# Reordering TensorE's work behind the state update of a hybrid DeltaNet and window-attention layer

## The chip, the cores and the metric

The kernel runs on one core of one Trainium2 chip. The metric is the device time of one execution in microseconds (us). Engines are named as in the profile: PE is TensorE (PEld its weight loads), DVE is VectorE, ACT is ScalarE, POOL is GpSimd, and SP issues most of the DMAs.

## What is computed

```python
h = rmsnorm(x, pre_norm_w)                      # x: 4096 rows of 1024, float32
proj = einsum('bsd,de->bse', h, w_in)           # 3336 columns
(qa, ka, va, za, ba, aa, qb, kb, vb, zb) = split(proj)
qkv = silu(causal_depthwise_conv(concat([qa, ka, va]), conv_w))
o_a = gated_deltanet(...)                       # 4 heads of 128, chunks of 64, state 128x128 a head
o_a = rmsnorm(o_a, dn_out_norm_w) * silu(za)
o_b = sliding_window_sink_attention(...)        # 8 heads of 64, window of 2 chunks
o_b = o_b * silu(zb)
y = einsum('bse,ed->bsd', concat([o_a, o_b]), w_out)
out = x + rmsnorm(y, post_norm_w)
```

## The kernel before

The 4096 rows are taken in 32 tiles of 128 rows (two chunks of 64). `run_steps` unrolls 33 steps for every engine; step t projects tile t (`proj`, the "fill") and mixes tile m = t - 1 (`mix`: DeltaNet, attention, output projection). It also prepares the x of tile t + 1 (`prep`). So step 0 has no mixing, steps 2 to 30 have all three parts, step 31 has a projection but no x to prepare, and step 32 has mixing alone. Step 1 (m = 0) also splits `w_out` into its half-precision parts, on ACT and DVE (`w_out_high`, `w_out_low`).

Each engine has its own program, and the order in it is written out by hand; engines meet at semaphores. `done(engine, event, n)` is a wait until `event` has come for tile n. On PE the work that depends on other engines is spread between pieces of the projection: `fill(n)` issues the next n of 26 pieces of tile t. A piece of the kind that matters here is 24 matmuls of 128 columns (L500), 8 chunks of the contraction by three products of high and low half-precision parts. The last four pieces are the columns of the DeltaNet queries (`FILL_Q`); their end releases `conv_fill` on ACT (L782 to L786), which feeds DVE's convolution of the queries (L1050, L1052), ACT's tanh (L792) and DVE's SiLU (L1061).

The end of a step on PE, in the order of the program (L680 to L718):

- the products of the state update: `per_head(2, k_tail, cw, ds_ready)` and `per_head(7, decay, cw, aw_ready)`, L515;
- `fill(2)`, then the output projection of group B's half: 24 matmuls of 512 columns into banks 4 and 5 (L692, from `out_b_half`);
- the four turns (transposes) of group A's normalised output `mt` into bank 3 (L708), which wait for `on_ready`; then `gate_columns` (L572);
- `fill(2)`, then `turn_x(t + 1)`: 16 turns of the high and low halves of the next x (L435), the second eight of which wait for `xl_ready`;
- the output projection of group A's half (L692, from `out_a_half`, whose buffer is `inv_t`), which waits for `out_a_ready` and signals `y_ready`.

`on_ready` is made by a chain over three engines that begins when the state update's products end: DVE adds the two parts of the output into `mt` (L1356); ACT squares and sums it per head (L947); DVE forms the argument (L1364, L1366); POOL takes the power (L1596), multiplies the four factors (L1598) and scales `mt` (L1600). Beside this chain DVE goes on in its own order: the last tap of the keys' convolution (L1052), then `low_half(t + 1)` (L1018, one pass over 1024 columns with two inputs in SBUF), then the gate of group B (L1069).

`out_a_ready` is made from the turned output: DVE multiplies by the gate (L1380), ACT copies to half precision (L957), DVE subtracts (L1387). In ACT's order `conv_fill(FILL_Q)`, the copy of the turned x (L752) and the queries' tanh come behind L957, and behind them the squares of the output projection (L966), which wait for `y_ready`. These lead over POOL (L1602 to L1606) to `y_rs` and to `finish` on DVE (L1400) in the next step.

At m = 0 one part of `w_out` (its chunk 4) lies for a while in the buffer `y_out`; DVE moves it away and signals `wo_ready` (L1031), and SP then loads the first rows of x into `y_out` (L407).

Of the kernel before, what the change touches and what calls it, by code (L numbers as in the profile page):

```python
# [87 lines left out]
def build(nc, x, pre_norm_w, w_in, conv_w, dn_a_log, dn_dt_bias, dn_out_norm_w, sw_sinks, w_out,  # L88
# [7 lines left out]
    with ExitStack() as ctx:  # L96
# [64 lines left out]
        out_b_half = sb("out_b_half", [128, 2, 4, 128], F16)  # L161
# [198 lines left out]
        @block.sync  # L360
        def _(sp):
            sp.dma_start(x_in[:, :], x[0, 0:TOK, :]).then_inc(x_loaded, 16)
            sp.dma_start(c32[:, :, :], const32).then_inc(const_loaded, 16)
            sp.dma_start(rows[0:48, :], conv_w[0].rearrange("k (b p) -> (k b) p", p=128)).then_inc(const_loaded, 16)
            sp.dma_start(rows[48:56, :], pre_norm_w[0].rearrange("(c p) -> c p", p=128)).then_inc(const_loaded, 16)
            sp.dma_start(rows[56:57, :], dn_out_norm_w).then_inc(const_loaded, 16)
            sp.dma_start(masks[:, :, :], const16).then_inc(const_loaded, 16)
            for c in range(NC):
                r = slice(128 * c, 128 * c + 128)
                for at, lo, hi in ((COL_Q, 0, 1536), (COL_ZA, 1536, 2048), (COL_QB, 2056, 2824),  # L370
                                   (COL_ZB, 2824, 3336), (COL_KVB + 256, 2048, 2056)):
                    sp.dma_start(w_raw[:, c + 1, at:at + hi - lo], w_in[0, r, lo:hi]).then_inc(w_loaded[c], 16)
            done(sp, xh_ready, 0)
            sp.dma_start(x_in[:, :], x[0, TOK:2 * TOK, :]).then_inc(x_loaded, 16)
            for c in range(NC):
                sp.dma_start(w_o[:, c, :], w_out[0, 128 * c:128 * c + 128, :]).then_inc(wo_loaded, 16)

            def step(t, p, mix, proj, prep):
                m = t - 1
                if mix:  # L380
                    done(sp, near_ready, m)
                    done(sp, xl_ready, t - 1 if proj else m - 1)
                    sp.dma_start(near_dram, m_near.rearrange("p h n -> p (h n)")).then_inc(near_stored, 16)
                    sp.wait_ge(near_stored, (m + 1) * 16)
                    sp.dma_start(x_in[:, 0:BLOCK * 4 * BLOCK],
                                 near_dram.rearrange("(b j) n -> b (j n)", j=BLOCK).unsqueeze(1).broadcast_to(
                                     [128 // BLOCK, BLOCK, 4 * BLOCK * BLOCK])).then_inc(block_loaded, 16)
                    sp.wait_ge(block_loaded, (m + 1) * 16)
                if proj:
                    done(sp, q_rot_ready, m)  # L390
                    sp.dma_start(rot_tab[:, :], rotary[bass.ds(t * TOK, TOK), :]).then_inc(rot_loaded, 16)
                if mix and m:
                    done(sp, post_ready, m - 1)
                    sp.dma_start(out[0, bass.ds((m - 1) * TOK, TOK), :], y_out[:, :]).then_inc(stored, 16)
                    sp.wait_ge(stored, m * 16)
                    sp.dma_start(y_out[:, :], x[0, bass.ds(m * TOK, TOK), :]).then_inc(res_loaded, 16)
                if not mix:
                    sp.wait_ge(w_hi_ready, 2 * NC)
                    sp.wait_ge(w_lo_ready, LOW_PARTS * NC)
                    done(sp, fill_ready[FILL_Q], 0)  # L400
                    sp.dma_start(post_w, post_norm_w.broadcast_to([128, D])).then_inc(pw_loaded, 16)
                if prep and mix:
                    done(sp, to_ready, m)
                    sp.dma_start(x_in[:, :], x[0, bass.ds((t + 1) * TOK, TOK), :]).then_inc(x_loaded, 16)
                if m == 0:
                    sp.wait_ge(wo_ready, 1)
                    sp.dma_start(y_out[:, :], x[0, 0:TOK, :]).then_inc(res_loaded, 16)  # L407

            run_steps(sp, step)
            done(sp, post_ready, NT - 1)  # L410
            sp.dma_start(out[0, bass.ds((NT - 1) * TOK, TOK), :], y_out[:, :]).then_inc(stored, 16)
            sp.wait_ge(stored, NT * 16)
# [3 lines left out]
        def _(pe):  # L416
# [8 lines left out]
            def turn_x(n):  # L425

                done(pe, xh_ready, n)
                done(pe, w_ready, n - 2)
                done(pe, o_ready, n - 2)
                for s in range(2):  # L430
                    if s:
                        done(pe, xl_ready, n - 1)
                    dst = bank[6 + s][:, :].bitcast(F16).rearrange("p (c n) -> p c n", c=NC)
                    for c in range(NC):
                        last = nc.tensor.transpose(dst[:, c, :], x_split(n)[:, s, 128 * c:128 * c + 128], ident16)  # L435
                last.then_inc(x_turned, 1)
# [38 lines left out]
            def step(t, p, mix, proj, prep):  # L475
                m = t - 1
# [3 lines left out]
                def fill(n, ahead=False):  # L480

                    nonlocal asked, issued
                    if not proj:
                        return
                    asked += 0 if ahead else n
                    while issued < (n if ahead else asked):
                        issued += 1
                        f, b = next(queue)
                        dst = bank[(p + f) % 2]
                        if (f, b) == (0, 0):  # L490
                            turned_x(pe, t)
                        if b == 0 and t == 1 and f < 2:
                            done(pe, fill_used[FIRST_USER[f]], 0)
                        elif b == 0:
                            done(pe, fill_used[(f - 2) % 7], t if f >= 2 else m)
                        if f in FILL_COL:
                            col = FILL_COL[f] + 128 * b
                            for c in range(NC):
                                for ws, xs in ((0, 0), (0, 1), (1, 0)):
                                    last = mm(dst[:, 128 * b:128 * b + 128], w_half[:, c, ws, col:col + 128],  # L500
                                              xt_half[:, xs, c, :], start=(c == 0 and ws + xs == 0),
                                              stop=(c == NC - 1 and ws == 1))
                        else:
                            col, n_col, per = (COL_QB, 512, NC // 4) if f == FILL_QB else (COL_KVB, KV, NC // 2)
                            for c in range(per * b, per * b + per):
                                for xs, ws in ((0, 0), (0, 1), (1, 0)):
                                    last = mm(dst[:, 0:n_col], xt_half[:, xs, c, :],  # L507
                                              w_half[:, c, ws, col:col + n_col], start=(c == 0 and ws + xs == 0),
                                              stop=(c == NC - 1 and xs == 1))
                        if (f, b + 1) not in PIECES:  # L510
                            last.then_inc(fill_ready[f], 1)
# [171 lines left out]
                done(pe, w_ready, m)  # L683
                per_head(2, k_tail, cw, ds_ready)
                per_head(7, decay, cw, aw_ready)
                fill(2)

                def project_out(chunks, src, begin, event=None):
                    for i, c in enumerate(chunks):
                        for xs, ws in ((0, 0), (0, 1), (1, 0)):  # L690
                            for n in range(2):
                                last = mm(bank[4 + n][:, :], src[:, xs, i, :],  # L692
                                          w_out_half(c, m)[:, ws, 512 * n:512 * n + 512],
                                          start=(begin and i == 0 and xs + ws == 0),
                                          stop=(not begin and i == len(chunks) - 1 and xs == 1))
                    if event is not None:
                        last.then_inc(event, 1)

                if m == 0:
                    pe.wait_ge(wo_lo_ready, 4)  # L700
                if m == 1:
                    pe.wait_ge(wo_ready, 1)
                project_out(range(4, 8), out_b_half, True)

                done(pe, on_ready, m)
                done(pe, qs_used, m)
                for h in range(4):
# [1 line left out]
                last.then_inc(o_turned, 1)  # L709
                if proj:  # L710
                    gate_columns(t)
                fill(2)
                if prep:
                    turn_x(t + 1)
                done(pe, out_a_ready, m)
                if m == 0:
                    pe.wait_ge(wo_lo_ready, NC)
# [955 lines left out]
```

## Time and profile before

| | |
|---|---|
| median of 3 runs | 2083.33 us (2082.55 to 2083.40) |
| span of the profiled execution | 2082.3 us |
| PE busy | 2008.8 us, 96% |
| PEld busy | 1666.1 us, 80% |
| DVE busy | 1612.2 us, 77% |
| ACT busy | 998.3 us, 48% |
| POOL busy | 525.7 us, 25% |
| DMA | 93.02 MB, mean 45 GB/s |

The profile is of one execution, whose span is 2082.3 us; the page gives no other time for it, and the median of the runs is 1.0 us above the span. A busy share counts the time in which an instruction of the engine is under way. The ends of matmuls are modelled, and the record of one overlaps the next by some tenths of a microsecond, so the beginning of the next instruction tells more than the recorded end. The chain that ended last, and the list of what ran at which time, show the order inside a step.

### The profile page before, as it was taken

The numbers are of one execution on the slowest core, as the hardware profiler recorded it, in microseconds if no ns is written. First come the engines' busy times: TensorE is split into PE (matmuls) and PEld (weight loads), VectorE is DVE, ScalarE is ACT, GpSimd is POOL, SyncE is SP. The second block draws the span as 40 slices with busy tenths as digits, with TensorE's granted clock in tenths as the row PEclk, the third lists the DMA queues.
The fourth block names the chain that finished last, engine by engine and source line by source line (L and its number), as shares of the span: only waits on it lengthen the run. The fifth ranks groups of instructions, "written<-read, shape, count | busy, mean of one in ns | idle before, by whom it ended". The sixth has DMA issues, their size and how long they took to land.

```text
span 2082.3 us, 61176 instructions
## 1 busy us (share of the span) xinstructions
PE 2008.8 (96%) x24913; PEld 1666.1 (80%) x24913; DVE 1612.2 (77%) x5455; ACT 998.3 (48%) x3144; POOL 525.7 (25%) x809
## 2 busy tenths in 40 slices
PE   7589999999999999999999999999999999999985
PEld 7568888888888888888878878888888888888873
DVE  6888777788777778777777877777877777887773
ACT  6655444545454544444454545454544444454532
POOL 0222222222222222222223222222222222322221
PEclk9799999999999999999999999999999999999996
DMA  9001100111110011110011111011111001111100
GB/s 359 27 23 54 44 24 23 43 45 44 44 34 23 33 44 44 44 44 24 23 43 44 44 44 34 18 38 44 44 44 41 19 30 44 45 44 44 33 10 34
DMA packets 35530, 93.02 MB, mean 45 GB/s; under 512 B 9209, under 2 KB 13618, under 8 KB 35250
## 3 DMA queue, kind: packets, MB, share of 16 engines
q1 hardware_dynamic: 34818, 89.11, 13.0%
q8 instruction: 197, 3.23, 0.7%
q14 instruction: 83, 0.68, 0.1%
q10 hardware_dynamic: 432, 0.01, 0.0%
HBM read 71.28 MB, written 17.83 MB: 43 GB/s over the span
## 4 chain that ended last, share of the span: by engine, by line
PE 89%; DVE 5%; ACT 3%; DMA 2%; issue 1%; SPq 0%; POOL 0%; POOLq 0%; ACTq 0%; DVEq 0%
PE bank L500 39%; PE bank L692 16%; PE bank L507 11%; PE bank L515 10%; PE bank L660 2%; PE bank L649 1%; PE bank L636 1%; DMA x_in<-near_scratch 1%; PE bank L435 1%; DVE w_raw L1435 1%; PE bank L555 1%; PE bank L532 1%; PE bank L537 1%; ACT w_raw L978 1%; PE bank L588 1%
## 5 line engine op out<-in xcount | busy, mean ns | idle before, releaser
L500 PE MATMUL bank<-xt_half,w_raw 128*128 128x128 f16 x14880 | 904.9, 219 | 9.6 <-ACT xt_half L752 9.6
L500 PEld LDWEIGHTS bank<-xt_half,w_raw 128*128 128x128 f16 x14880 | 863.6, 98 | 31.7 <-issue 15.5
L1052 DVE SCALAR_TENSOR_TENSOR qkv<-conv_in,cols,qkv 128x128 f32<-128x128 f32 x1152 | 391.8, 384 | 3.5
L507 PE MATMUL bank<-w_raw,xt_half 128*128 128x264 f16 (+1 forms) x1488 | 261.9, 330 | 2.0 <-DVE w_raw L1069 2.0
L507 PEld LDWEIGHTS bank<-w_raw,xt_half 128*128 128x128 f16 x1488 | 145.1, 98 | 87.1 <-DVE w_raw L1069 2.2
L692 PE MATMUL bank<-w_o,inv_t 128*128 128x512 f16 x768 | 172.7, 382 | 2.7 <-DVE inv_t L1387 2.7
L692 PE MATMUL bank<-w_o,out_b_half 128*128 128x512 f16 x762 | 169.7, 379 | 0.0
L692 PEld LDWEIGHTS bank<-w_o,inv_t 128*128 128x128 f16 x768 | 74.1, 98 | 87.5 <-DVE inv_t L1387 3.1
L1050 DVE TENSOR_SCALAR qkv<-conv_in,cols 128x128 f32<-128x128 f32 x384 | 90.9, 282 | 64.3 <-ACT halo L786 63.0
L692 PEld LDWEIGHTS bank<-w_o,out_b_half 128*128 128x128 f16 x762 | 73.2, 98 | 82.7
L752 ACT ACTIVATE xt_half<-bank,small 128x128 f16<-128x128 f16 x496 | 131.7, 418 | 3.8 <-DVE small L1479 3.6
L1142 DVE TENSOR_TENSOR masks<-x_in,base_inv 128x60 f32<-128x60 f32 (+14 forms) x480 | 108.9, 227 | 17.6 <-DMA x_in<-near_scratch 4.5
L1146 DVE TENSOR_TENSOR base_inv<-base_inv,masks 128x60 f32<-128x60 f32 (+14 forms) x480 | 106.3, 221 | 15.4
L792 ACT ACTIVATE tanh_c<-qkv 128x512 f32<-128x512 f32 x96 | 60.5, 630 | 113.4 <-DVE qkv L1052 113.3
L1602 POOL TENSOR_TENSOR small<-small 128x1 f32<-128x1 f32 x32 | 6.3, 196 | 404.7 <-ACT work L966 404.7
L1544 POOL TENSOR_TENSOR q_rot<-shared,rot_tab 128x512 f32<-128x512 f32 x32 | 41.4, 1294 | 224.1 <-ACT shared L825 224.1
L1380 DVE TENSOR_TENSOR bank<-bank,w_raw 128x512 f32<-128x512 f32 x32 | 22.4, 699 | 96.0 <-PE bank L708 96.0
L1596 POOL TENSOR_TENSOR small<-small 128x4 f32<-128x4 f32 x32 | 33.8, 1057 | 240.2 <-DVE small L1366 240.2
L782 ACT ACTIVATE conv_in<-halo 128x12 f32<-128x12 f32 x96 | 20.1, 209 | 153.1 <-PE bank L500 153.1
L1061 DVE SCALAR_TENSOR_TENSOR qkv<-tanh_c,qkv 128x512 f32<-128x512 f32 x96 | 66.1, 689 | 34.2 <-ACT tanh_c L792 34.1
L957 ACT ACTIVATE inv_t<-bank 128x512 f16<-128x512 f32 x32 | 19.1, 597 | 151.8 <-DVE bank L1380 151.8
L906 ACT ACTIVATE shared<-bank,small 128x128 f32<-128x128 f32 x256 | 89.6, 376 | 0.0
(257 smaller groups left out, 3546.0 us busy)
## 6 DMA issues: line engine op xcount, KB each, us to landing
x_in<-in_x_dram SPq DMA_DIRECT2D x32, 512.0 KB, 3.3
x_in<-near_scratch SPq DMA_DIRECT2D x32, 512.0 KB
y_out<-in_x_dram SPq DMA_DIRECT2D x32, 512.0 KB, 3.2
out_dram<-y_out SPq DMA_DIRECT2D x32, 512.0 KB, 2.9
w_raw<-in_w_in_dram SPq DMA_DIRECT2D x8, 768.0 KB, 10.8
w_raw<-in_w_in_dram SPq DMA_DIRECT2D x16, 256.0 KB, 10.9
w_o<-in_w_out_dram SPq DMA_DIRECT2D x8, 512.0 KB, 12.8
w_raw<-in_w_in_dram SPq DMA_DIRECT2D x8, 384.0 KB, 10.9
```

The lines of the kernel that those rows point to most:

```text
L500: last = mm(dst[:, 128 * b:128 * b + 128], w_half[:, c, ws, col:col + 128], xt_half[:, xs, c, :], start=(c == 0 and ws + xs == 0), stop=(c ...
L507: last = mm(dst[:, 0:n_col], xt_half[:, xs, c, :], w_half[:, c, ws, col:col + n_col], start=(c == 0 and ws + xs == 0), stop=(c == NC - 1 a ...
L515: last = mm(bank[b][:, 128 * h:128 * h + 128], lhs[:, h, :], right[:, h, :] if len(right.shape) == 3 else right, start=start, stop=stop)
L692: last = mm(bank[4 + n][:, :], src[:, xs, i, :], w_out_half(c, m)[:, ws, 512 * n:512 * n + 512], start=(begin and i == 0 and xs + ws == 0) ...
L752: last = f(xt_half[:, s, c, :], src[:, c, :], ACT.Identity, scale=x_factor[:, c:c + 1])
L792: f(tanh_c[:, :], qkv[:, 4 * g:4 * g + 4, :].rearrange("p h n -> p (h n)"), ACT.Tanh, scale=0.5).then_inc(tanh_c_ready[g], 1)
L906: last = f(soft[:, hh, :], heads(4 + hh // 4)[:, hh % 4, :], ACT.Exp, scale=DH_B ** -0.5, bias=row_max[:, hh:hh + 1], accum_out=row_sum[:, ...
L1050: last = v.tensor_scalar(dst, conv_in[:, b, 0:TOK], tap, None, ALU.mult)
L1052: last = v.scalar_tensor_tensor(dst, conv_in[:, b, i:i + TOK], tap, dst, ALU.mult, ALU.add)
L1061: v.scalar_tensor_tensor(y, tanh_c[:, :], 1.0, y, ALU.add, ALU.mult).then_inc(qkv_ready[g], 1)
L1142: link(v.tensor_tensor(x_prod[:, :, 0:k], m_block[:, 0:k, :, k].rearrange("p j h -> p h j"), base_inv[:, :, k:k + 1].broadcast_to([128, 4, ...
L1146: link(v.tensor_tensor(base_inv[:, :, 0:k], base_inv[:, :, 0:k], x_prod[:, :, 0:k], ALU.subtract))
```

## The change

PE's order at the end of a step is rewritten. All four last pieces of the projection stand directly behind the state update's products; then come the turns of group A's output, `gate_columns` and `turn_x`; both output projections stand last, one behind the other. Since group B's projection of m = 0, which reads `y_out`, now stands behind the turns, SP's load into `y_out` waits in addition for `y_ready` of tile 0.

```diff
                 if m == 0:
                     sp.wait_ge(wo_ready, 1)
+                    done(sp, y_ready, 0)
                     sp.dma_start(y_out[:, :], x[0, 0:TOK, :]).then_inc(res_loaded, 16)
...
                 per_head(7, decay, cw, aw_ready)
-                fill(2)
+                fill(4)
...
+                done(pe, on_ready, m)
+                done(pe, qs_used, m)
+                for h in range(4):
+                    last = nc.tensor.transpose(heads(3)[:, h, :], mt[:, h, :], ident)
+                last.then_inc(o_turned, 1)
+                if proj:
+                    gate_columns(t)
+                if prep:
+                    turn_x(t + 1)
                 if m == 0:
                     pe.wait_ge(wo_lo_ready, 4)
                 if m == 1:
                     pe.wait_ge(wo_ready, 1)
                 project_out(range(4, 8), out_b_half, True)
-
-                done(pe, on_ready, m)
-                done(pe, qs_used, m)
-                for h in range(4):
-                    last = nc.tensor.transpose(heads(3)[:, h, :], mt[:, h, :], ident)
-                last.then_inc(o_turned, 1)
-                if proj:
-                    gate_columns(t)
-                fill(2)
-                if prep:
-                    turn_x(t + 1)
                 done(pe, out_a_ready, m)
```

PE before, at the end of a step with all three parts. `xt_half` is the turned x, `w_raw` holds the weights, `out_b_half` and `inv_t` hold the halves of the mixed output, `mt` is group A's output before it is turned:

```order
L515 MATMUL bank<-cw,decay 128x128 x4
L500 MATMUL bank<-xt_half,w_raw 128x128 x48
L692 MATMUL bank<-w_o,out_b_half 128x512 x24
L708 MATMUL bank<-c,mt 128x128 x4
L572 MATMUL bank<-small,c 128x4
L500 MATMUL bank<-xt_half,w_raw 128x128 x48
L435 MATMUL bank<-masks,shared 128x128 x16
L692 MATMUL bank<-w_o,inv_t 128x512 x24
L588 MATMUL bank<-c,small 128x128 x4
```

And PE at the same place in the changed kernel, with the semaphores that stand ahead of an instruction (a group is then split at its first instruction):

```order
L516 MATMUL bank<-cw,decay 128x128 x4
L501 MATMUL bank<-xt_half,w_raw 128x128 [waits conv_in_ready1]
L501 MATMUL bank<-xt_half,w_raw 128x128 x95
L703 MATMUL bank<-c,mt 128x128 [waits qs_used,on_ready]
L703 MATMUL bank<-c,mt 128x128 x3
L573 MATMUL bank<-small,c 128x4 [waits state_ready,g_ready]
L436 MATMUL bank<-masks,shared 128x128 [waits o_ready,w_ready,xh_ready]
L436 MATMUL bank<-masks,shared 128x128 x7
L436 MATMUL bank<-masks,shared 128x128 [waits xl_ready]
L436 MATMUL bank<-masks,shared 128x128 x7
L693 MATMUL bank<-w_o,out_b_half 128x512 [waits wo_ready]
```

Between the state update and the turns of `mt` there are now 96 fill matmuls, where there were 48 and the 24 wide matmuls of group B's projection; that projection now stands behind all turns and directly ahead of group A's.

SP at m = 0, in the changed kernel; before, the row of `y_out` waited for `wo_ready` alone:

```order
L391 DMA rot_tab<-in_rotary_dram 128x128 [waits q_rot_ready,block_loaded]
L404 DMA x_in<-in_x_dram 128x1024 [waits base_made]
L408 DMA y_out<-in_x_dram 128x1024 [waits y_ready,wo_ready]
L383 DMA near_scratch<-masks 128x64 [waits xl_ready,near_made]
L385 DMA x_in<-near_scratch 128x1x1024 [waits near_stored]
```

No row of SP changes its place; the exchange through `near_scratch` of the next step is what is queued behind the longer wait.

## Rows read from the trace of the kernel before

**Rows 1.** The page: span, and busy time of PE (share, instructions).
```profile
span 2082.3 us, 61176 instructions
...
PE 2008.8 (96%) x24913; PEld 1666.1 (80%) x24913; DVE 1612.2 (77%) x5455; ACT 998.3 (48%) x3144; POOL 525.7 (25%) x809
```

**Rows 2.** Windows of the trace: length, busy time of each engine, granted clock, DMA.
```profile
core 0: us, PE busy (x) PEld busy (x) DVE busy (x) ACT busy (x) POOL busy (x), PEclk, DMA share, GB/s
240.00:1000.00 760.00, 759.57 (x9678) 630.68 (x9677) 596.14 (x2061) 364.61 (x1206) 200.93 (x312) 1.00 0.13 40
```

**Rows 3.** The chain that ended last, one step: start us, us, what.
```profile
1013.05 2.68 PE bank L500 x48
1015.73 5.18 PE bank L692 x24
1020.91 0.44 PE bank L708 x4
1021.35 0.12 PE bank L572 x2
1021.47 2.70 PE bank L500 x48
1024.16 0.89 PE bank L435 x16
1025.06 5.18 PE bank L692 x24
```

**Rows 4.** Timeline of POOL and DVE, same step: start, us, instruction, idle before, releaser.
```profile
1016.70 1.09 POOL L1598 TENSOR_TENSOR small<-small 128x4 f32<-128x4 f32 x1
1017.87 1.04 POOL L1600 TENSOR_TENSOR mt<-mt,small 128x512 f32<-128x512 f32 x1
...
1016.46 1.28 DVE L1018 SCALAR_TENSOR_TENSOR shared<-x_in,small,shared 128x1024 f16<-128x1024 f32 x1
...
1022.75 0.69 DVE L1387 TENSOR_TENSOR inv_t<-bank,inv_t 128x512 f16<-128x512 f32 x1
```

**Rows 5.** Line L1598 over the whole span: duration ns min/median/max, starts.
```profile
L1598 POOL TENSOR_TENSOR small<-small x32: 204/1092/1093, 154.1 to 2061.7; 128x4 f32<-128x4 f32 x32
```

**Rows 6.** Timeline of POOL in step 31, which prepares no x.
```profile
2002.64 0.20 POOL L1598 TENSOR_TENSOR small<-small 128x4 f32<-128x4 f32 x1
```

**Rows 7.** Timeline of step 1 (m = 0): PE, PEld and POOL.
```profile
149.41 2.84 PE L500 MATMUL bank<-xt_half,w_raw 128*128 128x128 f16 x48
...
157.31 0.42 PEld L708 LDWEIGHTS bank<-c,mt 128*128 128x128 f32 x4 [0.37 <-POOL mt L1600]
...
162.23 5.35 PE L692 MATMUL bank<-w_o,inv_t 128*128 128x512 f16 x24 [0.55 <-DVE inv_t L1387]
...
155.30 1.96 POOL L1600 TENSOR_TENSOR mt<-mt,small 128x512 f32<-128x512 f32 x1
```

**Rows 8.** Start of step 32 on PE and ACT, timeline.
```profile
2015.11 0.60 PE L588 MATMUL bank<-c,small 128*128 128x128 f32 x4
...
2016.05 0.58 ACT L966 ACTIVATE work<-bank 128x512 bf16<-128x512 f32 x1
```

**Rows 9.** End of step 32 on PE and POOL, timeline.
```profile
2057.91 5.34 PE L692 MATMUL bank<-w_o,out_b_half 128*128 128x512 f16 x24
...
2065.88 7.04 PE L692 MATMUL bank<-w_o,inv_t 128*128 128x512 f16 x24 [2.15 <-DVE inv_t L1387]
...
2061.97 1.04 POOL L1600 TENSOR_TENSOR mt<-mt,small 128x512 f32<-128x512 f32 x1
```

**Rows 10.** The chain that ended last, step 32: the turns of group A's output.
```profile
2063.25 0.49 PE bank L708 x4
```

**Rows 11.** Windows on PE: length, busy time, granted clock, DMA.
```profile
162.00:166.00 4.00, 3.77 (x18) 1.00 0.39 131
...
2067.00:2070.00 3.00, 3.00 (x8) 0.50 0.00 0
```

More of the change, by code:

```diff
@@ L697, in project_out @@
                         last.then_inc(event, 1)
[L699 to L703, printed above, removed]
                 done(pe, on_ready, m)
@@ L711, in step @@
                     gate_columns(t)
-                fill(2)
                 if prep:
                     turn_x(t + 1)
+                if m == 0:
+                    pe.wait_ge(wo_lo_ready, 4)
+                if m == 1:
+                    pe.wait_ge(wo_ready, 1)
+                project_out(range(4, 8), out_b_half, True)
                 done(pe, out_a_ready, m)
```

## The prediction

> **What bounds the kernel now.** I read the page first, for the engine that fills the span: PE is busy for 2008.8 of 2082.3 us [rows 1]. A busy PE need not be a PE that sets the time, so I then took windows: from 240 to 1000 us PE is busy for 759.57 of 760 us at a granted clock of 1.00, the 2.4 GHz level [rows 2]. In the steps with all three parts PE therefore never stands still, and the 73 us in which it is idle lie in the setup and in the last step. The chain that ended last shows the same from inside: in such a step it is PE alone, instruction behind instruction [rows 3]. Two things follow. Nothing can be won in the 29 steps 2 to 30 by moving PE's instructions, since none is added or removed and there is no wait to remove. And any wait that the new order makes on PE there goes into the time in full, 29 times over. So the question is only whether the events that PE meets are still early enough. For that I laid the timelines of POOL and DVE beside the chain [rows 4].
>
> **The change in steps 2 to 30.** PE's reference point is the end of the state update's products, 1013.05, where the first fill matmul starts [rows 3]. The same moment starts the chain DVE, ACT, DVE, POOL that makes `on_ready`.
>
> *The turns of group A's output.* POOL's scaling of `mt` ends at 1017.87 + 1.04 = 1018.91 [rows 4], which is 5.86 us behind the reference. From the end of that instruction to PE takes 0.05 us: in step 1 it ended at 155.30 + 1.96 = 157.26, and the weight load that waited for it began at 157.31 [rows 7]. So the turns can begin 5.91 us behind the reference. Before, 2.68 us of fill and 5.18 us of projection lay ahead of them, together 7.86 us [rows 3]: nearly 2 us to spare. Now 96 fill matmuls lie ahead, 2 x 2.68 = 5.36 us. PE comes 5.91 - 5.36 = **0.55 us** too early. Four turns behind a wait took 0.49 us [rows 10] against 0.44 us behind running work [rows 3], so I add 0.05 us for the restart. Against that, fill matmuls that follow fill matmuls save the 0.02 us by which the second 48 were slower than the first 48 [rows 3]. Net: 0.58 us a step.
>
> Can the chain itself move? Its start is PE's own, DVE and ACT were waiting for it, and all that DVE does beside it (the last tap, the low half of x, the gate) stands in the same order behind the same events. I take it as rigid. One link in it is soft: POOL's product of 128x4 elements takes 1.09 us where DVE is running the low half of x [rows 4], 1092 ns in the median step, 204 ns at best [rows 5], and 0.20 us in step 31, which has no low half [rows 6]. It ends just behind DVE's pass. That is 0.89 us that the chain loses to DVE, more than the whole stall. In the rival below this product comes first and the chain is 5.91 - 0.89 = 5.02 us long; here I keep 5.91, as the row has it.
>
> The Trainium skill (SBUF — State Buffer, section "SBUF: two separate sides") says of the port pair that VectorE and GpSimd share, for a VectorE instruction with two inputs in SBUF too, that whichever "starts first gets the pair for the whole instruction; the other fully blocks". By that rule the sum is the one above while the low half starts first, and that of the rival once POOL does; the trace agrees in that the product is long only where the low half began ahead of it.
>
> *The rest of PE's order.* `gate_columns` needs nothing late. The turns of the low half need DVE's pass, which ends by 1017.74 [rows 4], ahead of the turns of `mt`: covered. If it were not, it would be the next wait. Group B's projection needs its half, which was there 3 us earlier than it will now be read. Group A's needs `out_a_ready`: DVE's subtraction ended at 1023.44 [rows 4], 2.53 us behind the start of the turns at 1020.91 [rows 3]; now 0.44 + 0.12 + 0.89 + 5.18 = 6.63 us lie between the two. Covered by 4 us.
>
> *The other engines.* The queries' pieces end earlier against the next step by the projection that was between them, so ACT's copies and DVE's convolution of the queries start about 3 us earlier (ACT's order holds them behind its copy of `out_a`). That buys nothing where PE is the bound. `y_ready` still ends the step, and what follows hangs on it as before, the exchange through DRAM included.
>
> *SP.* The load of `y_out` waits some 8 us longer, once. Behind it is queued the exchange of step 2, which waits for DVE's work of that step anyway, and POOL's addition of the first rows follows only behind `finish` of step 2. I cost it at nothing; if that cover were gone it would be at most the few us of one load.
>
> 29 steps x 0.58 = **16.8 us**. Below, the stall is 0 if the link gives way; above, I allow 0.8 us a step, if the restart costs as much again or the chain is a little later than the rows have it.
>
> **Step 1.** DVE is clogged with `w_out`, and POOL's scaling ends late: the turns began at 157.31, 7.90 us behind the reference 149.41 [rows 7]. With 5.36 us of fill PE waits 2.5 us. It no longer waits the 0.55 us for `out_a_ready` [rows 7], and saves nothing else: **+2.0 us**. Bounds 1.5 and 2.5.
>
> **Step 31.** Without the low half the chain is 5.91 - 0.89 = 5.02 us [rows 6], less than 5.36: no stall. And here the earlier queries do pay. Before, their SiLU held DVE and their tanh held ACT: ACT's squares began at 2016.05, though PE had gone on to the next turns at 2015.11 [rows 8]. Step 32 is a serial run over all engines that starts from these squares. Now they start with PE: **-0.8 us** (0.94 less a tenth for PE's result to arrive).
>
> **Step 32.** There is no fill, so PE stands still from 2057.91 until POOL's scaling ends at 2061.97 + 1.04 = 2063.01, plus 0.05 [rows 9]: 5.15 us. Then 0.49 us of turns [rows 10] and both projections, 2 x 5.18 us [rows 3]: 16.0 us. Before, group B's projection filled the first wait, and from 2057.91 to the end of group A's, 2065.88 + 7.04, it was 15.0 us [rows 9]. So the new order loses 1.0 us at full clock. To that comes the clock. Before, group A's projection took 7.04 us instead of about 5.35 us, because after a wait of 2.15 us the granted clock was 0.50, the 1.2 GHz level, from 2067 to 2070 [rows 9, 11]: a price of 1.7 us. That is in both sums; behind an idle time of 5.15 us I expect a longer stretch at that level, 1.7 to 4.2 us (the upper end is most of one projection at half speed), and take 2.5. Together **+3.5 us**, between 1 and 5.
>
> **Sum.** 16.8 + 2.0 - 0.8 + 3.5 = 21.5 us on the span of 2082.3 us, 2103.8. The median of the runs stands 1.0 us above the span; on it the forecast is 2083.3 + 21.5 = **2104.8 us**, 1.0% slower. A measurement of this kernel can tell about 0.2% from no change, 4.2 us.
>
> **The rivals.**
>
> *The short product (not slower).* The low half starts at 1016.46, POOL's product at 1016.70 [rows 4]. If it slips by 0.24 us or more, POOL runs first, the chain is 5.02 us, the 29 stalls vanish and every step is 0.02 us faster: 2083.3 - 0.6 + 2.0 - 0.8 + 3.5 = 2087.4 us, at the rim of no change; with the last step at its lower bound, 2085. Against it: nothing that the change touches moves DVE against this chain, and the median over 32 steps equals the maximum within 1 ns [rows 5], so the race is not close to tipping. Chance 4%.
>
> *The clock falls at each stall.* A wait of 2.15 us was followed by 1.7 us lost [rows 9, 11]. If 0.6 us were enough, every step would lose that too: 2104.8 + 29 x 1.7 = 2154 us. Against it: behind the wait of 0.55 us at 162.23 [rows 7] the granted clock stayed 1.00 [rows 11]. Chance 3%.
>
> *The release is earlier than the recorded end.* Spans on POOL are rough. If `on_ready` came 0.3 us or more ahead of what the row says, a step would lose 0.28 us or less: 2096 us or below. Against it stand the 0.05 us of step 1. Chance 5%.
>
> *Something unseen,* such as code loading or a transfer that falls badly, either way: 3%.
>
> **How the numbers follow.** The forecast's case has 85%. Its own range is the stall between 0.4 and 0.75 us a step (11.6 to 21.8 us), with 4.7 us from the single steps, give or take 2: 2098 to 2111 us, and this holds well over 8 in 10 with nothing needed from the other cases. Chances: faster by over 0.2% 1%, within 0.2% 4%, slower 95%.
>
> **What would show it.** In windows of the steady steps PE busy should fall by about 1% of the time; the list of waits should show the turns of `mt` (L703) waiting for POOL's L1600 some 30 times, 0.5 to 0.6 us each and once 2.5 us; the step should last 0.6 us longer. POOL's product should still take 1.09 us in 29 steps. In step 32 PE should be idle for 5.1 us ahead of the turns and run slow behind them. ACT's L966 should start with PE at step 32. A list of waits without L1600, or a clock below 1.00 in the steady windows, would prove me wrong.

## The result and the profile after

The changed kernel takes 2111.44 us (median of 4 runs, 2109.64 to 2114.23) against 2083.36 us before (4 runs, 2082.55 to 2084.11): the ratio is 1.0136, with a 95% interval of 1.0124 to 1.0148. I had forecast 2104.8 us, between 2098 and 2111. The direction, the place and the mechanism of the steady steps were right; the loss was 28.1 us where I had summed up 21.5, and the result lies 0.4 us outside the range.

The profiled execution took 2111.02 us, with a span of 2109.2 us. The one behind the profile of before took 2084.11 us, with a span of 2082.3 us, so the two profiles differ by 26.9 us where the medians differ by 28.1. The page, with PE and the chain that ended last; POOL, which had no share in it before, now has 5%:

```profile
span 2109.2 us, 61177 instructions
...
PE 2013.7 (95%) x24913; PEld 1664.3 (79%) x24913; DVE 1614.7 (77%) x5455; ACT 990.7 (47%) x3144; POOL 525.0 (25%) x809
...
PE 82%; DVE 5%; POOL 5%; ACT 4%; issue 2%; DMA 2%; SPq 0%; POOLq 0%; ACTq 0%; DVEq 0%
```

Windows of the same stretch as in [rows 2] (length, busy time by engine, granted clock, DMA). PE is idle for 7.4 us where it was idle for 0.4, at a clock that is still 1.00:

```profile
240.00:1000.00 760.00, 752.63 (x9591) 624.71 (x9590) 588.74 (x2012) 354.42 (x1176) 199.75 (x306) 1.00 0.12 37
```

PE's waits from 240 to 1960 us (engine and line, waited for, total us, times, longest). The longest entry is the forecast stall, 0.56 us each time; the trace has it in each of the 29 steps 2 to 30:

```profile
PE bank L703 <- POOL mt L1599: 15.2, 27, 0.6
```

One such step, PE's timeline and POOL's (start, us, instruction, idle before):

```profile
1026.65 5.52 PE L501 MATMUL bank<-xt_half,w_raw 128*128 128x128 f16 x96
1032.73 0.66 PE L703 MATMUL bank<-c,mt 128*128 128x128 f32 x4 [0.56 <-POOL mt L1599]
1033.22 0.28 PE L573 MATMUL bank<-small,c 128*128 128x4 f32 x2
1033.37 1.05 PE L436 MATMUL bank<-masks,shared 128*128 128x128 f16 x16
1034.26 5.34 PE L693 MATMUL bank<-w_o,out_b_half 128*128 128x512 f16 x24
1039.44 5.34 PE L693 MATMUL bank<-w_o,inv_t 128*128 128x512 f16 x24
...
1030.47 1.09 POOL L1597 TENSOR_TENSOR small<-small 128x4 f32<-128x4 f32 x1
1031.63 1.04 POOL L1599 TENSOR_TENSOR mt<-mt,small 128x512 f32<-128x512 f32 x1
```

The wait of 0.56 us agrees with the forecast, and yet the step got longer by more. Measured from the first turn of a step to that of the next, before and after:

```profile
228.97 0.60 PE L588 MATMUL bank<-c,small 128*128 128x128 f32 x4
290.53 0.60 PE L588 MATMUL bank<-c,small 128*128 128x128 f32 x4
```

```profile
233.28 0.60 PE L589 MATMUL bank<-c,small 128*128 128x128 f32 x4
295.60 0.60 PE L589 MATMUL bank<-c,small 128*128 128x128 f32 x4
```

That is 61.56 us before and 62.32 us after; over all steps the medians are 61.55 and 62.33. The difference is 0.78 us a step, not 0.58. The missing 0.2 us is visible when the new rows are laid beside the old ones in the same view. The timeline of before has the first fill matmul, and DVE's first use of the products ahead of it, here:

```profile
1012.88 2.84 PE L500 MATMUL bank<-xt_half,w_raw 128*128 128x128 f16 x48
1013.09 0.69 DVE L1356 TENSOR_TENSOR mt<-mt,bank 128x512 f32<-128x512 f32 x1 [1.22 <-PE bank L515]
```

The fill began at 1012.88, while I had counted from 1013.05, where the chain of waits hands over to it [rows 3]. The two differ by 0.17 us, by which the record of the products ahead overlaps that of the fill; I call this stretch their drain. DVE, which needs their result, started behind it, at 1013.09, but PE had already begun to use up its cover at 1012.88. POOL's scaling ends 6.03 us behind that start (1018.91), and the turns follow 0.05 us later, so the chain is 6.08 us long. In the changed kernel it is the same: 1032.73 - 1026.65 = 6.08 us. The cover is 5.36 us, so the wait is 0.72 us. The view shows 0.56 of it, because the recorded 5.52 us of the fill have the drain in them too. The last 0.06 us are the restart: the turns behind the wait take 0.49 us to the next instruction (1032.73 to 1033.22), and 0.43 us before. Theory A of the experiments is this account. Its rival, theory B, is that the stall is 0.55 us and the new order itself costs the rest.

The other miss is step 1. Timeline of PE (the step began its fill at 149.49), and windows on PE (length, busy, granted clock, DMA):

```profile
157.38 0.66 PE L703 MATMUL bank<-c,mt 128*128 128x128 f32 x4 [2.37 <-POOL mt L1599]
...
158.90 2.76 PE L693 MATMUL bank<-y_out,out_b_half 128*128 128x512 f16 x6
...
165.77 5.34 PE L693 MATMUL bank<-w_o,inv_t 128*128 128x512 f16 x24
```

```profile
158.00:159.00 1.00, 1.00 (x20) 0.95 0.06 16
159.00:162.00 3.00, 3.00 (x10) 0.50 0.00 0
162.00:163.00 1.00, 1.00 (x6) 0.85 0.00 0
```

Behind a wait of 2.37 us the granted clock fell to 0.50, the 1.2 GHz level, for 3.4 us (the three microseconds at 0.50, and by the means of 0.95 and 0.85 a part of the ones beside them), and group B's projection took 165.77 - 158.90 = 6.87 us where it takes 5.18 us at 2.4 GHz: 1.7 us that my sum did not have.

### The profile page after: what moved, and what is told of

The parts are those of the page before. It is cut to its first block, busy times and chain, and to the rows that moved or that the text cites. A ratio compares the mean times of both kernels' runs of the same rounds, so it can differ in the third digit from the quotient of the medians.

```text
span 2109.2 us, 61177 instructions
## 1 busy us (share of the span) xinstructions
PE 2013.7 (95%) x24913; PEld 1664.3 (79%) x24913; DVE 1614.7 (77%) x5455; ACT 990.7 (47%) x3144; POOL 525.0 (25%) x809
## 4 chain that ended last, share of the span: by engine, by line
PE 82%; DVE 5%; POOL 5%; ACT 4%; issue 2%; DMA 2%; SPq 0%; POOLq 0%; ACTq 0%; DVEq 0%
PE bank L501 31%; PE bank L693 16%; PE bank L508 11%; PE bank L516 9%; ACT work L946 2%; PE bank L661 2%; POOL mt L1599 2%; POOL small L1597 2%; POOL small L1595 2%; PE bank L650 1%; PE bank L637 1%; PE bank L436 1%; DMA x_in<-near_scratch 1%; PE bank L703 1%; DVE mt L1355 1%
## 5 line engine op out<-in xcount | busy, mean ns | idle before, releaser
L965 ACT ACTIVATE work<-bank 128x512 bf16<-128x512 f32 x64 | 37.6, 593 | 138.5 <-PE bank L693 138.5
L1202 DVE COPY small<-bank 128x4 f32<-128x4 f32 x32 | 5.2, 163 | 120.3 <-PE bank L589 120.3
L881 ACT ACTIVATE w_raw<-bank 128x512 f32<-128x512 f32 x32 | 19.1, 597 | 139.9 <-PE bank L610 139.9
```

## The experiments

Three kernels first, to tell what the 0.78 us of a steady step are made of. The kernel before, run 11 times beside this group, took 2084.22 us in the median; the ratios are to it.

**Half the cover.** In `step` on PE, with `turn_x` split by halves:

```diff
+                if proj:
+                    gate_columns(t)
+                if prep:
+                    turn_x(t + 1, [0])
                 done(pe, on_ready, m)
...
-                if proj:
-                    gate_columns(t)
                 if prep:
-                    turn_x(t + 1)
+                    turn_x(t + 1, [1])
```

> The changed kernel, but the gate columns (0.14 us) and the eight turns of the high half of x (0.45 us) stand ahead of the turns of group A's output: 0.59 us more cover. Theory A (the stall is 0.72 us counted from the real start of the fill matmuls, which begin 0.17 us before the products ahead of them have drained): 0.13 us of wait is left, with the restart 0.18 us a step, 29 x 0.18 = 5.2 us above full_cover, some 2091 to 2093 us; PE's wait list shows the turns waiting in some 28 steps. Theory B (the stall is 0.55 us, as I forecast, and the rest of the loss is something else): no wait at the turns in steady steps, and a step that stays longer than before by the unexplained 0.2 us.

Measured: 2094.61 us, ratio 1.0053 (1.0038 to 1.0068). PE's timeline of one step:

```profile
1017.93 5.52 PE L503 MATMUL bank<-xt_half,w_raw 128*128 128x128 f16 x96
1023.29 0.34 PE L575 MATMUL bank<-small,c 128*128 128x4 f32 x2
1023.48 0.61 PE L437 MATMUL bank<-masks,shared 128*128 128x128 f16 x8
1024.02 0.66 PE L709 MATMUL bank<-c,mt 128*128 128x128 f32 x4
```

The turns of `mt` start 1024.02 - 1017.93 = 6.09 us behind the fill, exactly the chain of theory A, although the wait list names no wait there: what is left of it is shorter than the drain that the records show. So the list did not show the waits that I had expected in it, and the time is 1.6 us above the range that I gave. A step lasts 61.75 us in the median, 0.20 us above before. Taken by themselves, a list without the wait and a step longer by 0.20 us are also what theory B said; only the start at 6.09 us speaks for A here, and the next kernel has to decide.

**The full cover.** Gate columns and all of `turn_x` ahead of the turns of `mt`:

```diff
+                if proj:
+                    gate_columns(t)
+                if prep:
+                    turn_x(t + 1)
                 done(pe, on_ready, m)
...
-                if proj:
-                    gate_columns(t)
-                if prep:
-                    turn_x(t + 1)
```

> The changed kernel, but the gate columns and all 16 turns of the next x stand ahead of the turns of group A's output: 5.36 + 0.14 + 0.89 = 6.39 us of cover against a chain of 6.08 us. Theory A: no wait in steady steps, a step lasts 61.55 us as before, and only step 1 (+0.8 us, or +2.5 us if the clock still falls behind its wait of about 1.4 us) and steps 31 and 32 (+1.7 us) are left: 2086 to 2088 us. Theory B (0.2 us a step comes from the new order itself, for example from both projections back to back): 2092 to 2094 us.

Measured: 2088.57 us, ratio 1.0022 (1.0010 to 1.0033). A step:

```profile
229.81 0.60 PE L589 MATMUL bank<-c,small 128*128 128x128 f32 x4
291.43 0.60 PE L589 MATMUL bank<-c,small 128*128 128x128 f32 x4
```

61.62 us, 0.06 us above before: with the projections back to back as in the change, but no wait, nearly nothing of the 0.78 us is left. Theory B, which wanted 0.2 us a step and 2092 to 2094 us, falls. Half and full cover differ by 0.14 us a step in the medians, against the 0.18 us that theory A gave. The time is half a microsecond above the range of theory A, and the 0.06 us a step stay unexplained.

**The low half early.** On DVE, in the 1.2 us of idle time ahead of the state update's products:

```diff
+                if prep:
+                    low_half(t + 1)
                 if first:
                     w_out_low(4)
...
-                if prep:
-                    low_half(t + 1)
```

> The changed kernel, but DVE makes the low half of the next x ahead of its wait for the state update's products, in the 1.2 us in which it was idle. If POOL's small product is long only because DVE runs the low half at that time, it takes 0.20 us now, the chain is 5.2 us, below the cover of 5.36 us, and the stalls are gone: 2087 to 2090 us. Rival: the small product is long whatever DVE does, or another link grows: stalls stay, 2108 us or more.

Measured: 2091.15 us, ratio 1.0037 (1.0024 to 1.0049), a microsecond above the expected range; in step 1 the wait is 2.65 us here, not 2.37. POOL and PE of one step:

```profile
1018.34 0.20 POOL L1597 TENSOR_TENSOR small<-small 128x4 f32<-128x4 f32 x1
1018.62 1.05 POOL L1599 TENSOR_TENSOR mt<-mt,small 128x512 f32<-128x512 f32 x1
...
1014.52 5.52 PE L501 MATMUL bank<-xt_half,w_raw 128*128 128x128 f16 x96
1019.88 0.61 PE L703 MATMUL bank<-c,mt 128*128 128x128 f32 x4
```

POOL's small product went from 1.09 to 0.20 us, the turns start 5.36 us behind the fill, which is the fill itself, and a step lasts 61.56 us. So the product was long because of DVE's pass, and with that pass elsewhere PE's order of the change costs nothing in a steady step. The rule of the Trainium skill (SBUF — State Buffer, section "SBUF: two separate sides") that I had cited beside the sum agrees with this trace: with DVE's pass out of the way the product is 0.89 us shorter.

The next four put the new order into some steps only, and lengthen the wait. The kernel before, run 19 times beside this group, took 2083.63 us.

**Steady steps only.** `fill(4 if new else 2)`, and behind it the new order where `new = 1 < t < NT`, else the old one; SP without the added wait.

> The new order in steps 2 to 31, the old one in steps 1 and 32 (and SP without the added wait). Theory A gives 29 steps x 0.78 = 22.6 us, less 1.1 us by which step 32 starts sooner: 21.5 us above before, 2105 us. If most of what I missed lay in the steady steps' interplay with steps 1 and 32, it would be nearer 2100 or 2111 us. Step 1 and step 32 themselves should last as long as before.

Measured: 2106.53 us, ratio 1.0111 (1.0096 to 1.0126), so 20 to 26 us by the interval and 22.9 us by the medians; theory A's 21.5 lies inside. Most steps last 62.33 or 62.34 us. The steady steps carry about four fifths of the change's loss.

**Step 1 only.** `new = t == 1`.

> The new order in step 1 alone. In the trace of the changed kernel step 1 is 3.4 us longer: 1.8 us of wait that is left over and 1.7 us of a projection at half clock behind a wait of 2.4 us. Theory (the wait costs the clock): 2.5 to 4 us above before, group B's projection of step 1 takes some 6.9 us. Rival (the half clock there was chance): 1.8 us above before and 5.2 us for the projection.

Measured: 2086.93 us, ratio 1.0016 (1.0007 to 1.0026). Windows and timeline of PE behind the wait, again 2.37 us:

```profile
155.67 0.66 PE L705 MATMUL bank<-c,mt 128*128 128x128 f32 x4 [2.37 <-POOL mt L1615]
...
164.04 5.34 PE L694 MATMUL bank<-w_o,inv_t 128*128 128x512 f16 x24
```

```profile
156.00:157.00 1.00, 1.00 (x14) 0.78 0.06 16
157.00:158.00 1.00, 1.00 (x11) 0.50 0.00 0
...
159.00:160.00 1.00, 1.00 (x4) 0.51 0.00 0
```

The clock fell again, in another kernel at the same wait. Its half-speed stretch began about 0.6 us earlier behind the turns, so part of the price fell on the turns of x, and group B's projection took 6.28 us (from 157.76), not the 6.9 us that I expected. From the start of the fill to the next step's turns it is 21.44 us, as in the changed kernel. The time's interval, 1.5 to 5.4 us, holds both rivals; the windows decide for the first.

**Step 32 only.** `new = t == NT`.

> The new order in step 32 alone. Theory: PE idles 5.1 us ahead of the turns, then one projection runs partly at 1.2 GHz and the other at 2.4 GHz: 2.8 us above before. Rival (my forecast's longer stretch at half clock, 2.5 us): 3.5 us. The windows of the clock tell the two apart.

Measured: 2085.99 us, ratio 1.0016 (1.0007 to 1.0025). The times can't tell 2.8 from 3.5 us. PE's timeline can:

```profile
2066.42 0.83 PE L704 MATMUL bank<-c,mt 128*128 128x128 f32 x4 [5.00 <-POOL mt L1614]
2067.04 6.90 PE L693 MATMUL bank<-w_o,out_b_half 128*128 128x512 f16 x24
2073.78 5.34 PE L693 MATMUL bank<-w_o,inv_t 128*128 128x512 f16 x24
```

Turns and first projection together took 7.36 us instead of 5.67: 1.7 us lost behind an idle time of 5.00 us. That is the same price as behind 2.37 us in step 1 and behind 2.15 us before [rows 9, 11], so the longer stretch at half clock of my forecast did not come.

**A wait of two microseconds in every step.** `fill(3)` ahead of the turns, `fill(1)` behind the gate columns.

> The changed kernel, but only three pieces of the projection stand ahead of the turns, the fourth behind the gate columns: 4.02 us of cover, 1.34 us less. Theory A: the wait grows by as much to 2.06 us, a step lasts 63.7 us, and the time is 29 x 1.34 = 38.9 us above the changed kernel, 2150 us, if the clock holds. If a wait of 2.06 us costs the clock as the wait of 2.15 us did at the end of before, each step loses up to 1.7 us more: about 2200 us. If the extra 0.2 us a step were not part of the wait but of the order, the step would come out at 63.5 us.

Measured: 2183.68 us, ratio 1.0484 (1.0466 to 1.0501), 72.2 us above the changed kernel. Both predicted numbers are wrong, because both are right in part. Two steps that follow one another, each with the same wait, up to their ends (windows on PE: length, busy, granted clock, DMA):

```profile
998.97 0.84 PE L703 MATMUL bank<-c,mt 128*128 128x128 f32 x4 [1.90 <-POOL mt L1600]
...
999.89 2.72 PE L501 MATMUL bank<-xt_half,w_raw 128*128 128x128 f16 x24
...
1013.81 0.60 PE L589 MATMUL bank<-c,small 128*128 128x128 f32 x4
...
1064.27 0.66 PE L703 MATMUL bank<-c,mt 128*128 128x128 f32 x4 [1.90 <-POOL mt L1600]
...
1064.90 1.50 PE L501 MATMUL bank<-xt_half,w_raw 128*128 128x128 f16 x24
...
1077.49 0.60 PE L589 MATMUL bank<-c,small 128*128 128x128 f32 x4
```

```profile
1000.00:1002.00 2.00, 2.00 (x22) 0.50 0.00 0
...
1066.00:1068.00 2.00, 2.00 (x29) 1.00 0.03 8
```

In the second step the clock held: 1077.49 - 1013.81 = 63.68 us, the 63.7 us of theory A (62.33 + 1.34). In the first it fell, and such a step lasts 65.30 us in the trace, 1.62 us more. The waits explain 29 x 1.34 = 38.9 us of the 72.2. Followed step by step, the granted clock is at 0.50 behind the turns in 19 of the 29 steps, which makes 19 x 1.62 = 30.8 us. Of the last 2.5 us, 1.2 are a new wait in step 31 (61.89 us instead of 60.66), and the rest lies in irregular steps. I had treated the fall as a matter of yes or no by the length of the wait. Here it comes in two of three equal waits. What decides between them I have not tested.

Two of the last three kernels look for a version that is better than both; the third takes step 31 by itself. The kernel before, run 21 times beside them, took 2084.70 us.

**Both repairs.** New order in steps 2 to 31 with the low half early there, old order and old place in steps 1 and 32.

> A version meant to beat both: the new order in steps 2 to 31 with the low half of x early on DVE, the old order (and the low half in its old place) in steps 1 and 32. No stall in steady steps (61.56 us each), and step 32 starts about 0.7 us sooner behind PE: 1 us below before, which a measurement of this kernel can hardly tell from no change; a result 2 us or more above before would mean that a cost of the new order is still unexplained.

Measured: 2083.84 us (11 runs), ratio 0.9998 (0.9989 to 1.0007). No loss is left. The microsecond of gain is within what such a measurement can't tell.

**The kernel before with the low half early.**

> The kernel before with nothing but the low half of x early on DVE. The chain to the turns becomes 0.9 us shorter where the old order has 2 us to spare, so the time should not move: 2083 to 2084 us, a step of 61.55 us. A gain would mean that PE in the old order waited for something that the profile does not show.

Measured: 2083.53 us (10 runs), ratio 0.9996 (0.9987 to 1.0005), a step of 61.55 us in the median. A chain that is 0.9 us shorter where there is room of nearly 2 us gives nothing.

**Step 31 only.** `new = t == NT - 1`.

> The new order in step 31 alone, which has no low half of x and so no stall. PE's step 31 lasts as long as before, but ACT's squares at the start of step 32 follow PE's last projection within 0.2 us, not 0.94 us, and DVE's finish of the step starts 0.7 us sooner after it: about 1 us less in steps 31 and 32 together.

A single run, 2084.91 us, says nothing at this size. The trace shows the start of step 32:

```profile
2015.79 0.60 PE L588 MATMUL bank<-c,small 128*128 128x128 f32 x4
...
2019.94 3.65 PE L515 MATMUL bank<-qkv 128*128 128x128 f32 x16 [2.67 <-DVE shared L1414]
...
2015.99 0.60 ACT L980 ACTIVATE work<-bank 128x512 bf16<-128x512 f32 x1 [3.27 <-PE bank L693]
```

ACT's squares follow PE by 0.20 us, where it was 0.94 us [rows 8], and PE's next products by 4.15 us, where it was 4.87 us (2015.11 to 2019.98). So the 0.7 us at the start of step 32 are real and come from step 31 alone. They did not reach the end of this trace: from 2015.79 to its end it takes 67.3 us, and 67.2 us before. The microsecond that I expected of steps 31 and 32 together is not there. In the two kernels that also have the new order in step 31 and the old one in step 32, but change the steps ahead of them too (steady steps only, both repairs), the same stretch takes 65.8 us. The clock is a part of this difference: behind the same wait of 2.67 us it fell here and stayed up in the changed kernel. Windows on PE, this kernel and then the changed one:

```profile
2020.00:2023.00 3.00, 3.00 (x15) 0.52 0.00 0
```

```profile
2044.00:2050.00 6.00, 3.88 (x46) 1.00 0.03 5
```

## Why the prediction was right and where it fell short

**The bound and the kind of loss: right.** PE set the steady steps, nothing could be won there, and the one event that came too late was `on_ready`. The list of waits names it, with the number I gave. Taking the wait away, in two independent ways (more cover, or a shorter chain), brings the step back to 61.62 and 61.56 us.

**The stall's size: the step "PE's reference point is the end of the state update's products, 1013.05".** That is the reference of the chain, not of the cover. The cover starts with PE's next matmul, 1012.88, and the two differ by the drain of 0.17 us. For step 1 I had counted from the timeline's start, 149.41 [rows 7], and there the wait came out right; the sum of the steady steps mixed the two views. The stall is 0.72 us, with the restart 0.78 a step; 29 steps make 22.6 us instead of 16.8. These 5.8 us alone would have put the forecast at 2110.6. The timeline of the kernel before held all of this; I had read the start of the fill from the chain of waits, where each piece begins at the modelled end of the last.

**Step 1: the size of the wait right, its consequence left out.** The wait was 2.37 us in the list and 7.89 - 5.36 = 2.53 us from start to start (forecast 2.5). The step got 3.4 us longer: from the start of the fill to the next step's turns 170.95 - 149.49 = 21.46 us, before 167.42 - 149.41 = 18.01 us. Half of that is the clock, though I had priced just this fall for step 32, from a shorter wait, on the same page. The upper bound of 2.5 us was too low for the same reason.

**Step 31 into 32: right at its start, open at its end.** I had 0.8 us, and the first products of step 32 come 0.7 us sooner behind its first turns. From these turns to the last state update products it is 40.73 us in the changed kernel's trace and 41.90 us before, 1.2 us less. That is the number of one pair of traces and partly luck: the eight traces with the new order in step 31 have 40.5 to 42.0 us there, the four with the old one 41.3 to 42.1. The clock did not fall at the start of this step in the changed kernel; with step 31 alone changed it did, behind the same wait.

**Step 32: right in kind, a little too dear.** From its last state update products (2057.01 before, 2081.08 after) to the end of the span it takes 28.12 us against 25.29: 2.8 us, where I had 3.5. PE's idle time was 4.99 us in the list (forecast 5.15, counted from a start). The term that was mis-sized is the 2.5 us for the clock: the stretch at half clock was no longer than behind the shorter waits and cost 1.7 us. With the 1.0 us at full clock that is 2.7 us, against the 2.8 measured.

**The sum.** 22.6 + 3.4 - 1.2 + 2.8 = 27.6 us, against 26.9 us between the two spans. The rest lies in a few irregular steps: in the trace of before, four of them are together about 2 us longer than the median, in that of after about 1.2 us. PE waits there for the softmax, which stands behind the exchange through DRAM in the chain of such a step. How much they add differs from trace to trace, whatever the order: 1.2 us with the change, 2.1 before, 5.2 with the new order in step 32 alone.

**The rivals.** The short product did not come by itself, but where DVE's pass was moved it came, with the full 0.89 us: the mechanism existed, its condition did not. That the product is long only where the low half began ahead of it does not hold in step 1: there the product starts at 154.13, ahead of the low half (155.08), and takes 1.09 us beside a pass over `w_out` with two inputs in SBUF, which began at 153.89 (L1027). The clock stayed at 1.00 behind 0.56 us in the steady windows, as the wait of 0.55 us before had it. The SP queue's longer wait showed no cost: step 2 lasts 62.33 us like the steps behind it. The rival of an earlier release was the wrong way round: the stall was longer than the rows that I used, not shorter.

**The range.** I had allowed 0.4 to 0.75 us for the stall and 2 us either way for the single steps, as if the unknowns were in the durations. They were in the bookkeeping between two views. The measured stall of 0.78 lies just above the range's upper end. The text ahead of it allows 0.8 us a step, and the range does not use that; even its own terms, 2083.3 + 21.8 + 4.7 + 2, add up to 2111.8 and not to 2111.

## What to carry to other kernels

When cover is weighed against a chain on other engines, take both from the same kind of record: the cover from the start of one instruction to the start of the next on its own engine, and the chain from the same start, so that the wait for the end of the result is part of the chain. In this kernel the start of the next matmul and the end of the result lie 0.17 us apart, and a wait that is shorter than that did not even appear in the list of waits. And price every wait of about two microseconds on TensorE for the clock too, not only the longest: 1.7 us if it falls, and it is not certain to fall.

## What the hardware did that I had not expected

The price of a fallen clock hardly depended on the idle time ahead of it: 1.7 us behind 2.15, 2.37 and 4.99 us, and 1.6 us behind 1.90 us. In each of these cases the stretch at half clock lasted 3.4 us.

The length of the wait alone did not decide whether the clock fell. It never fell in 29 steps behind 0.56 us and fell in 19 of 29 behind 1.90 us. In step 1 of the half cover PE waited 1.73 us at the turns and the clock held (timeline, and window on PE):

```profile
157.23 0.66 PE L709 MATMUL bank<-c,mt 128*128 128x128 f32 x4 [1.73 <-POOL mt L1603]
```

```profile
155.00:165.00 10.00, 8.27 (x53) 1.00 0.01 2
```

The clock held behind longer waits too. Behind 2.67 us at the start of step 32 it held in the changed kernel and fell with step 31 alone changed, as shown above. With the low half early it even held behind a wait of 3.01 us in step 1:

```profile
126.92 1.09 PE L650 MATMUL bank<-c,shared 128*128 128x128 f32 x8 [3.01 <-ACT shared L913]
```

```profile
124.00:131.00 7.00, 4.08 (x46) 1.00 0.07 12
```

So a single trace says of such a wait what happened once. No run here separates what else decides.
